# Layer three's linear attentions: four of the matmul groups in each asked for one weight unit later

## The reference, cut to what matters

```python
def step(state, inp):
    qc, kc, vc, gc = inp
    b = jnp.cumsum(gc, axis=2)
    o_inter = jnp.einsum('bhtk,bhkv->bhtv', qc * jnp.exp(b), state)
    diff = jnp.where(causal, b[:, :, :, None, :] - b[:, :, None, :, :], -jnp.inf)
    scores = jnp.einsum('bhtsk,bhsk->bhts', qc[:, :, :, None, :] * jnp.exp(diff), kc)
    o_intra = jnp.einsum('bhts,bhsv->bhtv', scores, vc)
```

## Time and profile before

| | us |
|---|---|
| median of 3 runs (2251.71 to 2253.06) | 2251.89 |
| the profiled execution, its own time | 2253.25 |
| its span, first to last instruction | 2251.4 |
| TensorE matmul busy | 2239.0 (99%) |
| VectorE busy | 1561.8 (69%) |
| ScalarE busy | 1302.1 (58%) |

### The profile page before, as it was taken

How to read it: one execution, slowest core, us unless ns; L and a number is a source line. 1 busy time by engine, 2 the same in 40 slices (tenths; PEclk the granted TensorE clock), 3 DMA queues, 4 the chain that set the end, 5 groups by cost and what they waited for, 6 DMA issues and landing times.

```text
span 2251.4 us, 35131 instructions
## 1 busy us (share of the span) xinstructions
PE 2239.0 (99%) x14029; PEld 2016.6 (90%) x14029; DVE 1561.8 (69%) x1784; ACT 1302.1 (58%) x1752; POOL 12.8 (1%) x18
## 2 busy tenths in 40 slices
PE   9999999999999999999999999999999999999998
PEld 8899998888999988889999999988999999998887
DVE  6577577775775777788787577866766666665555
ACT  6455576454555764666765467555655556554444
POOL 0000000000000000000000000000000000000000
PEclk9999999999999999999999999999999999999999
DMA  9655558676546584656566656685666666667664
GB/s 330 209 166 169 179 179 280 232 235 199 168 155 187 193 296 153 224 190 190 181 199 191 187 170 197 211 281 197 198 205 202 197 203 204 200 224 240 204 202 146
DMA packets 130532, 460.04 MB, mean 204 GB/s; under 512 B 13848, under 2 KB 20544, under 8 KB 128448
## 3 DMA queue, kind: packets, MB, share of 16 engines
q1 hardware_dynamic: 129376, 451.43, 61.8%
q0 software_dynamic: 848, 6.30, 0.8%
q10 hardware_dynamic: 144, 0.07, 0.0%
HBM read 449.35 MB, written 8.40 MB: 203 GB/s over the span
## 4 chain that ended last, share of the span: by engine, by line
PE 95%; DVE 2%; ACT 1%; DMA 1%; issue 1%; SPq 0%; DVEq 0%; ACTq 0%
PE banks L317 91%; PE banks L417 1%; PE banks L402 1%; PE banks L448 1%; PE banks L381 1%; DVE wl L663 1%; PE banks L409 0%; DMA w_bc<-in_norm_mix_post 0%; ACT wh L491 0%; DMA early<-in_kv_t 0%; DVE lacc L824 0%; DVE lscore_lo L836 0%; PE banks L425 0%; DVE b L861 0%; DVE x_buf L956 0%
## 5 line engine op out<-in xcount | busy, mean ns | idle before, releaser
L663 DVE TENSOR_TENSOR wl<-raw,wh 128x1024 fp32r<-128x1024 f32 x774 | 940.8, 1223 | 465.6 <-ACT wh L491 463.3
L491 ACT ACTIVATE wh<-raw 128x1024 fp32r<-128x1024 f32 (+1 forms) x777 | 812.6, 1052 | 486.0 <-PE banks L317 416.1
L317 PE MATMUL banks<-xx,wh 128*128 128x512 f32 (+1 forms) x3760 | 856.8, 380 | 0.0
L317 PEld LDWEIGHTS banks<-xx,wh 128*128 128x128 f32 (+1 forms) x3760 | 690.0, 189 | 91.1 <-issue 1.0
L317 PEld LDWEIGHTS banks<-xx,wl 128*128 128x128 f32 x3712 | 455.2, 192 | 13.3
L317 PE MATMUL banks<-xx,wl 128*128 128x256 f32 x3712 | 465.2, 277 | 0.0
L317 PE MATMUL banks<-wh,xx 128*128 128x512 f32 x1504 | 360.4, 381 | 0.0
L317 PEld LDWEIGHTS banks<-wh,xx 128*128 128x128 f32 x1504 | 283.1, 189 | 39.0
L317 PE MATMUL banks<-wl,xx 128*128 128x512 f32 x752 | 196.2, 379 | 0.0
L317 PEld LDWEIGHTS banks<-wl,xx 128*128 128x128 f32 x752 | 142.4, 189 | 19.9
L317 PE MATMUL banks<-wh,yy 128*128 128x512 f32 x416 | 98.5, 379 | 0.0
(11 more groups left out here) (291 smaller groups left out, 1777.1 us busy)
## 6 DMA issues: line engine op xcount, KB each, us to landing
raw<-in_w_in_f SPq DMA_DIRECT2D x304, 512.0 KB, 3.6
raw<-in_w_ffn_f SPq DMA_DIRECT2D x160, 512.0 KB, 3.9
raw<-in_w_ffn_down SPq DMA_DIRECT2D x88, 512.0 KB, 4.4
raw<-in_w_in_t SPq DMA_DIRECT2D x80, 512.0 KB, 3.5
raw<-in_w_out_t SPq DMA_DIRECT2D x64, 512.0 KB, 4.6
raw<-in_w_o_t SPq DMA_DIRECT2D x32, 512.0 KB, 4.8
raw<-in_kv_f SPq DMA_DIRECT2D x16, 512.0 KB, 4.0
raw<-in_w_up_a_f SPq DMA_DIRECT2D x16, 512.0 KB, 3.5
```

The costliest lines, as they stand in the source:

```text
L317: return self.e.matmul(bank, stationary, moving, start=start, stop=stop, skip_group_check=True)
L491: self.e.activation(hi, source, ACT.Copy).then_inc(done.sem, 1)
L663: self.e.tensor_tensor(lo, source, hi.bitcast(f32), ALU.subtract).then_inc(done.sem, 1)
```

## The change

It adds one empty step at four places, for the attentions with `a.both` False alone, which are those of layer three: ahead of `across_halves`, ahead of the merged `level` of 8 and 4, ahead of that of 2 and 1, and ahead of `mean_squares`. No instruction is added or removed.

```diff
                 if not a.both:
-                    yield
+                    for _ in range(2):
+                        yield
                 tok = after(leveled)
                 x.across_halves(a, d, bank_free[6] + bank_free[7], tok)
...
-                    if group[0] > 8 and not a.both:
+                    if not a.both:
                         yield
                     toks = afters(leveled, len(group))
...
                 x.split_squares(a, (sq[1], tok), h, l)
                 yield
+                if not a.both:
+                    yield
                 tok = after(meaned)
                 x.mean_squares(a, (h, l, co[1], t_exact), (), tok)
```

## The result

The changed kernel takes 2263.44 us (median of 6 runs, 2262.34 to 2263.82) against 2251.89 us before: 11.55 us more. The ratio is 1.0049, with a 95% interval of 1.0039 to 1.0059, so it is slower. The profiled execution took 2262.34 us, the shortest of the six, with a span of 2260.5 us against 2251.4.

The account below looks back on a forecast made before the run. The prediction took TensorE, busy 2239.0 of 2251.4 us, to bound the kernel. Two added waits less those removed, 4.1 + 4.75 - 0.8 = +8.1 us, moved the median from 2251.9 to 2260.0 us, range 2257.7 to 2264.8.

Parts of the forecast that it names:

- The count of steps: Layer three's two attentions: 49 steps each become 53, 106 on 96 units, leaving 10 for the loop ahead of Fox columns.
- The first wait: At the second attention's linear_values, right behind unit 96: TensorE waits 4.1 us for the split's differences.
- T: End of the second attention's level of 2 and 1, where unit 96 starts; the linear_values chain is timed from it.
- The second wait: At the second attention's mean_squares, directly behind linear_values: TensorE waits 4.75 us, formerly hidden by three units.
- The waits removed: At across_halves (line 425) and the level of 2 and 1 (line 448): at most 0.8 us gone.
- The sum of the waits: Whole kernel: 4.1 + 4.75 - 0.8 = +8.1 us on the profiled execution.
- The clock: TensorE's granted clock during the two waits: main case has it stay at 1.00, adding nothing.
- The prediction's own sign of being wrong: Signs against it included PEclk under 1.00 after 1220, weight units between linear_values and mean_squares, or TensorE waits under 6 us.
- my second rival: Clock falls during the two waits: 2.3 us per recovery, 2262.3 us with one or 2264.6 with two; chance 0.25.
- the main case: Whole kernel: two waits and no more, median 2260.0 us; chance 0.61.
- Late engines after the loop: Roots, norm and first Fox scores crowd ScalarE and VectorE at unit 100; TensorE waits 1 to 3 us; chance 0.10.
- Later pay-back: From the attentions to the end: nothing can repay the loss, TensorE having one more wait, 0.6 us for xl.

Follow-up runs that it names:

- e5_fill: Changed kernel plus matmuls that nothing needs, 16 ahead of the second attention's linear_values and 18 ahead of its mean_squares; 2260.01 us against 2252.02 for the kernel before.
- e9_first_21_only: Kernel before plus one empty step, ahead of the merged level of 2 and 1 in the first attention alone; 2251.20 us against 2251.89.
- e2_across_84: Changed kernel cut to two empty steps per attention, ahead of across_halves and the merged 8 and 4; 2258.80 us against 2252.35 for the kernel before.
- e7_before_late_loop: Kernel before, with the loop that ends the second attention moved behind the second Fox attention's three column blocks; 2252.06 us against 2252.02.
- e10_late_loop_two: Finishing loop moved later, empty steps only ahead of across_halves and the merged 2 and 1 in both attentions; 2251.87 us against 2251.89 for the kernel before.
- e3_without_mean: Changed kernel without the empty step ahead of mean_squares, three of four kept in both attentions; 2264.11 us against 2252.35 for the kernel before.

## Why the prediction was right or wrong

**The count of steps: right.** 49 and 49 before, 53 and 53 after, on 96 units. `mean_squares` stands right behind `linear_values`, and that behind unit 96. The sums of 100, 102, 104 and 106 steps each gave the order on TensorE that the count says.

**The first wait: right.** 4.1 us foreseen; 4.1 from unit 96's end (1217.6) to `linear_values` (1221.7), of which the profile writes 3.89 as a wait. The two value copies and the split behind them took the places worked out: with T at 1214.93, the copies were to end at 1219.0 and the differences at 1221.6, and they ended at 1219.1 and 1221.5 in the changed kernel:

```profile
1217.83 1.26 ACT L628 ACTIVATE v<-banks,st 128x512 f32<-128x512 f32 x2 [3.79 <-PE banks L317]
...
1220.25 1.28 DVE L836 TENSOR_TENSOR lscore_lo<-lacc,lscore_hi 128x512 fp32r<-128x512 f32 x2
```

**The second wait: right.** 4.75 foreseen; in e5_fill, with the clock at 1.00, `mean_squares` starts 4.7 us after the end of `linear_values` (1224.10 to 1228.79).

**The waits removed: right in kind.** Both are gone. The stretch from the start of layer three (the matmuls of line 387, at 923.26 before and 922.79 after) to the end of unit 96 went from 299.2 to 294.8 us. Of the 4.4 us less, 3.2 are `linear_values` and `mean_squares`, which now stand behind unit 96, so it became 1.2 us shorter in itself, somewhat more than the 0.8 us. In e9_first_21_only the 0.6 us at line 448 went without a new wait in layer three, but its 0.7 us less cannot be told from none.

**The sum of the waits: right.** +8.1 foreseen; e5_fill, in which the clock is held and the waits remain, is 8.0 above its kernel before. From the start of layer three to the first Fox scores, the profiled execution of the changed kernel takes 10.4 us more than that of the kernel before (922.79 to 1235.01 is 312.2, 923.26 to 1225.09 is 301.8). Less 2.7 for the clock, that is 7.7.

**The clock: wrong, and it is the term that was put at nothing.** The step that failed is "5.0 us of rest did not lower it there, and both waits are shorter", from the tail. The clock fell although the rests were shorter: in e2_across_84 some 4 us into the only long rest, in the changed kernel 1.5 us after work had resumed from the first one. A rest that did not lower the clock once does not bound what another one does. The prediction's own sign of being wrong, a PEclk under 1.00 after 1220, came true, and TensorE's busy time, foreseen at 2239, read 2241.1. The fall of the clock was my second rival, with 0.25 where it deserved most of the chance; it gave 2262.3 for one recovery and 2264.6 for two, and the measured 2263.44 lies between. Its price was mis-sized too: 2.3 us for one recovery, from 5 us of opening matmuls. In the changed kernel the clock stayed at 0.50 for 10 us with one fall, and that cost 2.7 us by the rows and 3.6 by the medians; in e2_across_84, 2.9 and 3.0. The rule of the Trainium skill (TensorE: Matmul & The Clock Gate, "Why this matters for your kernels"), that pauses shorter than the tail's 5.0 us may bring the array back to half speed when they lie between bursts of matmuls, is borne out by the 0.50 of these windows. So the result lies in the range by some luck: the main case, 2260.0, is 3.4 us too low, and the upper end came from longer chains (+12.7), which did not come, or from two falls of the clock at 2.3 us each, where the profiled execution shows one fall at a higher price.

**Late engines after the loop: did not come.** Behind unit 97 no wait of TensorE stands in the rows of the changed kernel, and the first Fox scores follow at 1235.01.

**Later pay-back: small.** I said that nothing later could pay it back save the one wait for `xl`, 0.6 us. This wait is absent in the changed kernel's profiled execution. It is also absent in e7_before_late_loop and present in e10_late_loop_two, so it goes neither with the change nor with the later loop. That it comes and goes with the execution is likely, but no kernel has two profiles that would show it.

## What to carry to other kernels

Where small work is tied to the units of large work, count the steps against the units before a step is added: here one more step in each attention cost almost nothing, and the next one a whole chain of three engines. A helper that finishes what is left has to stand where its result is needed, and as late as the buffers allow. In a kernel bound by TensorE, price a pause of some 4 us with the clock in it: here 8.0 us of waits cost 11.5.

## What was not expected of the hardware

The granted clock can fall while matmuls run. In the changed kernel it drops at about 1223.2, in the midst of `linear_values`, 1.5 us after the rest. In e3_without_mean, the same order on TensorE, it fell at about 1221.6, at the end of the first rest, rose at about 1225.0, while the matmuls of `lacc` ran, and fell once more at about 1228.5, in the second rest:

```profile
1217.00:1223.00 6.00, 2.10 (x10) 1.68 (x10) 3.35 (x7) 2.82 (x5) 0.00 (x0) 0.89 0.25 87
1223.00:1226.00 3.00, 2.78 (x16) 2.58 (x15) 0.00 (x0) 0.19 (x1) 0.00 (x0) 0.66 0.00 0
1226.00:1229.00 3.00, 0.00 (x0) 0.00 (x0) 0.15 (x1) 2.82 (x5) 0.00 (x0) 0.91 0.56 175
1229.00:1231.00 2.00, 0.78 (x2) 0.71 (x3) 1.08 (x1) 0.00 (x0) 0.00 (x0) 0.50 0.00 0
```

The same two waits thus meet the clock in more than one way. The runs of the changed kernel also lie in two groups, 2262.3 to 2262.5 (mean clock 0.997) and 2263.3 to 2263.8 (0.996). Whether the groups are these two ways is open. Only profiled executions have windows, and the mean clock doesn't tell: that of e3_without_mean, with two falls, is 0.997 at 2264.11 us, and the changed kernel's, with one fall, 0.997 at 2262.34.
